# Attention over new and cached window values on one TensorE: one accumulation group per batch entry and head in place of two passes over the bank

## What is computed

```python
def swa_sample(h, buf, wqkv, bqkv, sinks, wo, bo):
    ...
    vc = jnp.concatenate([buf[:, :, 1], v], axis=1)      # 128 cached rows, then 4 new rows of values
    qg = q.reshape(b, t, SWA_KV_HEADS, SWA_GROUP, SWA_HEAD_DIM)
    sc = jnp.einsum('bthgd,bshd->bhgts', qg, kc).astype(jnp.float32) * SWA_SCALE
    ...
    p = sink_softmax(sc, sink).astype(vc.dtype)
    o = jnp.einsum('bhgts,bshd->bthgd', p, vc).reshape(b, t, SWA_HEADS * SWA_HEAD_DIM)
    ...
    return o @ wo + bo, state
```

## Time and profile before

| | us |
|---|---|
| median of 3 executions | 1926.85 |
| lowest, highest | 1917.56, 1930.35 |
| the profiled execution | 1926.85 |
| its span on the core | 1925.2 |
| PE busy | 1675.2 (87%) |
| mean granted TensorE clock | 0.912 of full |

### The profile page before, as it was taken

How to read it: one execution, slowest core, us unless ns; L and a number is a source line. 1 busy time by engine, 2 the same in 40 slices (tenths; PEclk the granted TensorE clock), 3 DMA queues, 4 the chain that set the end, 5 groups by cost and what they waited for, 6 DMA issues and landing times.

```text
span 1925.2 us, 27975 instructions
## 1 busy us (share of the span) xinstructions
PE 1675.2 (87%) x9304; PEld 875.3 (45%) x9305; DVE 555.5 (29%) x1508; ACT 409.1 (21%) x869; POOL 249.2 (13%) x350
## 2 busy tenths in 40 slices
PE   6799989999966898898988699999589899898885
PEld 3455557665543444443433244455344444444332
DVE  2333344333241111111111166665311111111113
ACT  2122224443111111111111123343011111111112
POOL 1132001341001111111111120000101111111100
PEclk9898989999977999999988799999699898999988
DMA  4243103674348999999999760030699999999983
GB/s 151 70 131 105 67 4 111 222 256 171 155 164 324 404 408 416 409 406 410 404 410 411 299 230 1 18 133 34 253 375 416 412 416 411 409 403 401 404 357 147
DMA packets 83608, 516.29 MB, mean 268 GB/s; under 512 B 22745, under 2 KB 41130, under 8 KB 57066
## 3 DMA queue, kind: packets, MB, share of 16 engines
q1 hardware_dynamic: 61962, 461.35, 60.0%
q0 software_dynamic: 21568, 53.93, 8.5%
HBM read 508.03 MB, written 26.52 MB: 278 GB/s over the span
## 4 chain that ended last, share of the span: by engine, by line
PE 73%; DMA 8%; issue 8%; DVE 5%; ACT 3%; DVEq 1%; SPq 1%; ACTq 0%; POOLq 0%; POOL 0%
PE ps L1866 64%; PE ps L1871 9%; DMA mem<-in_moe_w_up 4%; DMA mem<-in_cache_mla 1%; DVE mem L1525 1%; DMA mem<-in_x_sample 1%; DMA mem<-moe_rows_in,mem 1%; ACT mem L937 1%; ACT mem L721 1%; DMA mem<-moe_rows_back 1%; SPq L435 0%; DVE mem L1644 0%; DMA moe_rows_back<-mem 0%; DVE mem L1249 0%; ACT mem L865 0%
## 5 line engine op out<-in xcount | busy, mean ns | idle before, releaser
L1866 PE MATMUL ps<-mem 128*64 128x512 f32 (+16 forms) x7296 | 1429.9, 491 | 119.9 <-issue 48.6
L1866 PEld LDWEIGHTS ps<-mem 128*64 128x64 f32 (+5 forms) x7296 | 642.1, 151 | 818.6 <-issue 725.6
L1871 PE MATMUL ps<-mem 128*128 128x128 f32 (+2 forms) x2008 | 285.7, 282 | 122.6 <-DVE mem L1525 45.9
L721 ACT ACTIVATE mem<-ps 128x512 f32<-128x512 f32 (+4 forms) x367 | 198.7, 552 | 832.2 <-PE ps L1866 528.1
L1871 PEld LDWEIGHTS ps<-mem 128*128 128x128 f32 (+2 forms) x2008 | 240.2, 171 | 222.7 <-issue 194.3
L1525 DVE TENSOR_TENSOR mem<-mem,ps 64x512 f32<-64x512 f32 x64 | 44.2, 690 | 472.5 <-ACT mem L937 472.5
L650 POOL DMA_INDIRECT mem<-moe_rows_in,mem x70 | 65.3, 934 | 562.7 <-issue 539.1
L1536 DVE COPY mem<-ps 64x512 f32<-64x512 f32 x64 | 44.4, 693 | 308.3 <-PE ps L1866 308.3
L660 POOL DMA_INDIRECT moe_rows_back<-mem x64 | 59.0, 922 | 351.2 <-DVE mem L1536 344.5
L937 ACT ACT_TABLE_LOAD x32 | 41.1, 1283 | 221.8 <-PE ps L1866 221.8
L937 ACT ACTIVATE mem<-ps 64x512 f32<-64x512 f32 x64 | 37.6, 588 | 198.8 <-PE ps L1866 198.4
(11 more groups left out here) (219 smaller groups left out, 473.5 us busy)
## 6 DMA issues: line engine op xcount, KB each, us to landing
mem<-in_moe_w_gate SPq DMA_DIRECT2D x64, 2048.0 KB, 18.2
mem<-in_moe_w_up SPq DMA_DIRECT2D x64, 2048.0 KB, 24.1
mem<-in_moe_w_down SPq DMA_DIRECT2D x64, 2048.0 KB, 22.5
mem<-in_cache_mla POOLq DMA_DIRECT2D x160, 160.0 KB, 4.6
mem<-in_cache_mla SPq DMA_DIRECT2D x96, 160.0 KB, 5.5
mem<-moe_rows_back SPq DMA_DIRECT2D x8, 1024.0 KB, 8.9
mem<-in_mla_wo SPq DMA_DIRECT2D x1, 4096.0 KB, 13.5
moe_rows_in<-mem POOLq DMA_DIRECT2D x8, 512.0 KB, 2.9
```

The lines of the kernel that those rows point to most:

```text
L721: return act.activation(out, in_, ACT.Copy)
L1866: return pe.matmul(out, lhsT, rhs, start=start, stop=stop)
L1871: return pe.transpose(out, in_, ident[at:at + n, at:at + n])
```

## The change

The two passes become one. For each group, and in it for each sequence, the kernel issues the matmul over the cached values with 16 moving columns, which starts the accumulation, and right after it one over the new values, now with the 16 columns of this sequence alone, which ends it. The loop over groups is the outer one, that over sequences the inner one. Waits before, signal after, operands in memory and the places of the results are the same.

```diff
                         for g in range(SKV):
-                            to, at = slice(g % 2 * SD, (g % 2 + 1) * SD), g // 2 * NB * SG * NT
-                            mm(ps[to, 4, at:at + NB * SG * NT].rearrange("p (b r) -> p b r", b=NB), vb[0:NS, PT, g * SD:(g + 1) * SD],
-                               pTn_z[0:NS, :, g * NS:g * NS + SG * NT], g < 2, False)
-                        for b in range(NB):
-                            for g in range(SKV):
+                            for b in range(NB):
                                 to = slice(g % 2 * SD, (g % 2 + 1) * SD)
                                 at = (g // 2 * NB + b) * SG * NT
-                                last = mm(ps[to, 4, at:at + SG * NT], vbuf[:, b, g * SD:(g + 1) * SD],
-                                          pT_z[:, b, g * NS:g * NS + SG * NT], False, b == NB - 1 and g >= 2)
+                                rows = slice(g * NS, g * NS + SG * NT)
+                                mm(ps[to, 4, at:at + SG * NT], vbuf[:, b, g * SD:(g + 1) * SD], pT_z[:, b, rows], True, False)
+                                last = mm(ps[to, 4, at:at + SG * NT], vb[0:NS, PT, g * SD:(g + 1) * SD], pTn_z[0:NS, b, rows],
+                                          False, True)
                         last.then_inc(sig["z_mm"], 1)
```

## The result

| | us |
|---|---|
| median before, 6 executions | 1926.3 |
| median after, 6 executions | 1941.41 (1938.54 to 1944.14) |
| ratio after / before, 95% interval | 1.0087 (1.0063 to 1.011) |
| span of the profiled execution, before / after | 1925.2 / 1940.1 |

The changed kernel is slower by 0.87%: 15 us by the difference of the medians, 17 us by the ratio. The forecast was 1947, +19.8 us.

The account below looks back on a forecast made before the run. PE's chain was taken to bound the kernel. Block 20.4 us (4.0 at full clock, 16.4 at half) plus 2.0 after it less 2.56 gave +19.8 us on 1926.85, so 1947; range 1935 to 1954.

Parts of the forecast that it names:

- The place and the chain: Edited block at 1318.71 to 1321.27 us lies on PE's chain; time lost there moves the rest one for one.
- its own case: Edited block: shape changes cost time and the clock falls; 1943 to 1952 us, chance 0.68.
- rival 1: Edited block: shape changes cost as forecast but the clock stays up; +11.3 us, so 1938, chance 0.15.
- A change of shape breaks the stream at each call: Edited block: each alternation of 128 and 32 rows breaks the stream; 0.217 us a call, 13.9 us for 64 calls.
- Rival 2: Edited block: alternating shapes cost nothing, only halves' turns are lost; +4.9 us, 1932, or +9.2 with clock fall; chance 0.09.
- rival 3: Edited block: loads run far ahead, both halves stay busy and breaks vanish; +2 us, 1929, chance 0.03.
- The halves no longer take turns: Edited block: 16 calls in a row go to one column half; a 0.058 us step yields one record, not two.
- The clock falls: PE drops from 2.4 to 1.2 GHz about 4 us after the edited block starts.
- Full-clock part: Start of the edited block: 4.0 us at full clock hold 18.4 calls.
- A call at half clock: Later part of the edited block: 0.36 us a call, 45.6 calls in 16.4 us.
- Slow tail: After the edited block: 4 us at half clock lose half, 2.0 us.
- Rival 4: Expert stage after the block: its transfers go ahead of PE, so a later PE does not matter; 1927, chance 0.03.

Follow-up runs that it names:

- r3: Changed kernel with the second call of each pair over the 128 cached rows again, new keys left out; block +5.1 us, ratio to before 1.005.
- r4: Changed kernel with two groups at a time, so the shape changes once for two calls on different column halves; block +6.5 us, ratio to before 1.0042.
- r2: Changed kernel's 64 calls in two passes, cached first, group as inner loop so column halves take turns; block +1.9 us, ratio to before 1.002.
- r9: Changed kernel with 128 moving columns a call, all calls over the 32 new rows, cached keys left out; block +19.8 us, ratio to before 1.0104.
- r5: Changed kernel with 64 moving columns in each call instead of 16; block +19.7 us, ratio to before 1.0135.
- r6: Changed kernel with 128 moving columns in each call instead of 16; block +32.1 us, ratio to before 1.0149.
- r8: Changed kernel with 128 moving columns a call, all calls over the 128 cached rows, new keys left out; block +10.3 us, ratio to before 1.0058.

## Why the prediction was right, point by point

- **The place and the chain** held. The block is on the chain, no other engine got a new wait, and SP's issue, the norm's stores and the gather came later by what PE lost. DVE's copies ended at 1335.22 and were used at 1344.23, so they still have slack.
- **The time** came out below the range of its own case. The forecast gave shape changes with a fall of the clock 1943 to 1952; the median is 1941.4, between that and the 1938 of rival 1. The time alone could not have told the two apart. The block's length and its clock do.
- **Counts** held: 64 load records over 32 rows, 64 over 128 (two of the 66 are of `values`).
- **A change of shape breaks the stream at each call** held. Price foreseen: 0.217 us a call at full clock. Measured: 27 matmul records of 16 columns started in the first 2.90 us (the rows by shape below), 13.5 calls, 0.215 us each. r3 and r4 show that it hangs on the change of shape. Rival 2 (no price when alternating) is refuted by r3 against the change (+5.1 and +16.6 us in the block), rival 3 with it. The Trainium skill (TensorEngine Tiling, "Key Properties") has a change of mode drain the engine, and gives no duration. This trace agrees: a call with its change took 0.215 us. Weight loads pulled ahead of the matmuls did not hide these breaks: in the same 2.90 us the weight unit was busy for 2.54.

```profile
L1866 PE MATMUL ps<-mem 128*64 128x16 f32 x14 | 2.0, 216 | 0.0
L1866 PE MATMUL ps<-mem 32*64 32x16 f32 x13 | 2.0, 219 | 0.0
L1866 PE MATMUL ps<-mem 128*64 128x128 f32 x6 | 0.5, 273 | 0.0
```

- **The halves no longer take turns** held, as a smaller part: r3, which has only this and the calls, costs +5.1 us in the block, where r2, with turns, costs +1.9.
- **The clock falls** held, which rules out rival 1. The Trainium skill (TensorE: Matmul & The Clock Gate, "Loop structure matters more than you think") has back-to-back matmuls stay warm. This case does not bear that out: in r9 PE was busy for 2.80 of 2.80 us and then for 19.30 of 19.30, and the clock was 0.50 in the second stretch.
- **The sum's terms.** Full-clock part: foreseen 4.0 us with 18.4 calls, measured 2.9 with 13.5. A call at half clock: foreseen 0.36, measured 0.320; that is the term that was sized most wrongly. I scaled the whole call by ratios of 1.62 and 1.71 from rows that hold no change of shape; the call with its change grew by 0.320 / 0.215 = 1.49. The two errors were opposite, and that was luck: 50.5 calls at 0.320 are 16.2 us, where 45.6 at 0.36 were foreseen, 16.4. The block was foreseen at 20.4 us and took 19.3 (1314.30 to 1333.64). Slow tail: its 4.0 us at 0.50 came as foreseen, but they cost 1.5 us and not half of 4. Together 19.8 foreseen and 18.1 in the rows; the medians and the ratio give 15 to 17, with an interval of 12 to 21 us.
- **Rival 4** (the expert stage swallows it) is refuted: SP's issue shifted with PE, and the stage behind it was 1.0 us longer, not shorter.
- **Its reason for the fall was only half right.** "The new block streams half as many columns for its time" named the columns alone. That it gave the right answer here was in part luck: carried to r2, r5 and r6 it gave the wrong one. All of these have 32-row calls, and r9 against r8 shows that such calls count less for the clock; that this is why r2, r5 and r6 fell is likely and was not shown by a run of its own.

## What to carry to other kernels

Count the changes of array shape in the order in which small matmuls are issued. Here a call with its change took 0.215 us, against 0.12 on one half without a change and 0.06 with the halves in turn, and inside the block two passes have one change where the interleaved order has 63. Group calls by shape, and inside a shape let successive calls take turns on the column halves. A run of some microseconds of small matmuls, here above all over few rows, can halve TensorE's clock though the engine shows 100% busy, and the matmuls after it pay too; read the granted clock beside the busy share.

## What the runs showed of the hardware that I had not expected

- An engine busy all the time over 32 rows by 64 columns of the array, with 128 moving columns a record, was put from 2.4 to 1.2 GHz 2.9 us after it began (r9); over 128 rows by 64 it ran 13.0 us at 2.4 GHz (r8). The moving values of r9 are mostly zeros, and the effect of that was not separated.
- The row count has no price at full clock (19 loads of 128-column calls in 2.10 us over 128 rows and over 32).
- At half clock a call with its change of shape took 0.320 / 0.215 = 1.49 times as long, an unbroken record of 128 columns over 1.8 times as long (11 loads in 2.21 us, where 19 had taken 2.10).
- On one half a record of 16 columns took twice as long (0.058 us, r3) as with the halves in turn (0.030, r2), though the engine counts as busy in both.
